# Where VectorE copies the second transposed block in a windowed attention: after the maxima of both heads, or between them

## The reference

```python
proj = h @ w_in                      # q: 16 heads of 64, k and v: 4 heads of 64, z: 1024
s = einsum(q, k) / 8                 # blocks of 128 queries against the block before and their own
s = where(in_band, s, -inf)          # diff >= 0 and diff < 128
m = maximum(max(s), sink)            # one sink per head
p = exp(s - m)
p = p / (sum(p) + exp(sink - m))
o = einsum(p, v)
return (o * silu(z)) @ w_out
```

## Time and profile before

| | |
|---|---|
| time, median of 3 runs | 1680.35 us (1679.25 to 1680.95) |
| time of the profiled execution | 1681.84 us |
| its span, first to last instruction | 1680.0 us |
| PE busy | 1616.8 us (96%) |
| DVE busy | 935.2 us (56%) |
| ACT busy | 707.2 us (42%) |
| slots i = 2 to 7 | 84.35 to 157.06 us of the span, six of 12.12 us |

### The profile page before, as it was taken

One profiled execution on the slowest core, in us unless ns is written; L12 is line 12 of the kernel. 1 busy time (PEld: TensorE's weight loads), 2 busy tenths in 40 slices (PEclk: granted clock), 3 DMA queues, 4 the chain that ended last, 5 costly groups with the idle time before them and its releaser, 6 DMA issues.

```text
span 1680.0 us, 20851 instructions
## 1 busy us (share of the span) xinstructions
PE 1616.8 (96%) x7745; PEld 1290.7 (77%) x7745; DVE 935.2 (56%) x1583; ACT 707.2 (42%) x1268; POOL 139.1 (8%) x131
## 2 busy tenths in 40 slices
PE   5998999999999999999999999999999999999998
PEld 4866888877778567888888888778566888888886
DVE  6566557566666765543434346566766643434343
ACT  4356532545544654422323244454664532323232
POOL 3000222031500001100000011000000200000001
PEclk8999999999999999999999999999999999999999
DMA  4211223323121101333333232211201232333331
GB/s 135 85 40 51 86 90 101 100 88 101 51 76 51 51 26 54 110 101 101 100 99 101 75 100 91 85 51 51 76 26 51 93 109 76 104 97 100 100 100 50
DMA packets 127271, 135.62 MB, mean 81 GB/s; under 512 B 2442, under 2 KB 120788, under 8 KB 127188
## 3 DMA queue, kind: packets, MB, share of 16 engines
q1 hardware_dynamic: 126084, 133.19, 24.7%
q0 software_dynamic: 288, 1.05, 0.2%
q10 hardware_dynamic: 816, 0.30, 0.1%
HBM read 132.43 MB, written 2.10 MB: 80 GB/s over the span
## 4 chain that ended last, share of the span: by engine, by line
PE 75%; DVE 14%; ACT 5%; issue 4%; DMA 1%; POOL 1%; SPq 0%; DVEq 0%; POOLq 0%; ACTq 0%
PE U L1228 21%; PE U L1230 21%; PE U L1229 21%; DVE cc L914 3%; PE Z L1406 3%; PE O L1460 2%; DVE ea L916 2%; DVE ea L911 1%; DVE pr L815 1%; PE U L1271 1%; PE U L1272 1%; PE U L1273 1%; DVE pr L833 1%; DMA raw<-in_attn_w_in 1%; PE O L1454 1%
## 5 line engine op out<-in xcount | busy, mean ns | idle before, releaser
L1228 PE MATMUL U<-XH,WL 128*128 128x512 f32 x976 | 386.3, 396 | 6.1 <-issue 5.2
L1230 PE MATMUL U<-XH,WH 128*128 128x512 f32 x976 | 381.3, 391 | 0.0
L1229 PE MATMUL U<-XL,WH 128*128 128x512 f32 x976 | 380.9, 390 | 0.0
L765 DVE TENSOR_TENSOR WL<-raw,WH 128x1024 fp32r<-128x1024 f32 x246 | 313.2, 1273 | 62.4 <-ACT WH L500 55.8
L500 ACT ACTIVATE WH<-raw 128x1024 fp32r<-128x1024 f32 x246 | 257.1, 1049 | 210.9 <-PE U L1230 173.6
L1228 PE MATMUL U<-MH,WL 128*128 128x512 f32 x848 | 335.7, 396 | 1.9 <-DVE tb L1097 1.7
L1230 PE MATMUL U<-MH,WH 128*128 128x512 f32 x848 | 330.8, 390 | 0.0
L1229 PE MATMUL U<-ML,WH 128*128 128x512 f32 x848 | 330.1, 389 | 0.0
L1228 PEld LDWEIGHTS U<-XH,WL 128*128 128x128 f32 x976 | 183.9, 188 | 44.6 <-issue 7.0
L1230 PEld LDWEIGHTS U<-XH,WH 128*128 128x128 f32 x976 | 183.7, 188 | 38.9
L1229 PEld LDWEIGHTS U<-XL,WH 128*128 128x128 f32 x976 | 184.0, 189 | 36.2
(11 more groups left out here) (219 smaller groups left out, 1756.4 us busy)
## 6 DMA issues: line engine op xcount, KB each, us to landing
raw<-in_w_ff SPq DMA_DIRECT2D x64, 1024.0 KB, 5.2
raw<-in_w_in SPq DMA_DIRECT2D x24, 1024.0 KB, 5.1
raw<-in_attn_w_in SPq DMA_DIRECT2D x10, 1024.0 KB, 5.3
raw<-in_pool_w_in SPq DMA_DIRECT2D x8, 1024.0 KB, 5.4
raw<-in_w_o SPq DMA_DIRECT2D x8, 1024.0 KB, 5.2
raw<-in_attn_w_out SPq DMA_DIRECT2D x4, 1024.0 KB, 5.0
raw<-in_pool_w_out SPq DMA_DIRECT2D x4, 1024.0 KB, 5.1
xin<-in_x SPq DMA_DIRECT2D x2, 1024.0 KB, 7.8
```

Source lines behind the costliest of these rows:

```text
L765: v.tensor_tensor(w_slot(WL, t, shape), src, w_slot(WH, t, shape).bitcast(F32), ALU.subtract).then_inc(lo_done, 1)
L1228: mm(o, wl, xh, start=first, stop=False, **kw)
L1229: mm(o, wh, xl, start=False, stop=False, **kw)
L1230: return mm(o, wh, xh, start=False, stop=last, **kw)
```

## The change

VectorE's copy of the second round of transposes moves from behind the maxima of both heads to between them: first the maxima of head 0, then the copy, then the maxima of head 1. No instruction is added or removed; the wait on the negated maxima of both heads and the release of the scores' PSUM stay behind head 1.

```diff
-            def swa_softmax_a(st):
+            def swa_softmax_a(st, heads):
                 j = st["pair"]
                 dve.wait_ge(z_done, st["zd"] + 1)
                 if j >= 2:
                     dve.wait_ge(p0_done, swa_t_of[j - 2]["p0"] + 4)
-                for i in range(2):
+                for i in heads:
...
-                dve.wait_ge(negm_ready, 2 * j + 2)
-                dve.sem_inc(z_free, 1)
+                if 1 in heads:
+                    dve.wait_ge(negm_ready, 2 * j + 2)
+                    dve.sem_inc(z_free, 1)
...
                 if "swa_qk" in by_op:
-                    swa_softmax_a(by_op["swa_qk"])
+                    swa_softmax_a(by_op["swa_qk"], [0])
                 if "swa_t" in by_op:
                     swa_evict(by_op["swa_t"], 1)
+                if "swa_qk" in by_op:
+                    swa_softmax_a(by_op["swa_qk"], [1])
                 conv(s["t"] + 2)
```

## The result

The changed kernel takes 1687.5 us in the median of 5 runs (1684.54 to 1689.87), the kernel before beside it 1680.35 us (1678.42 to 1681.16): 7.2 us more, a ratio of 1.005 with a 95% interval of 1.0039 to 1.0062. The direction was as forecast, the size was not: 4.3 us and at most 1686.8 us had been predicted. A second set of runs, made with the experiments, gave 1690.13 against 1678.87 us (1.0069, 1.0056 to 1.0082).

A forecast was written before the change was run, and what follows sets the result against it. The prediction took VectorE's ordered list, not TensorE, to set the slots' pace. Six slots of 0.72 us gave 4.3 us, so 1680.35 became 1684.7 us, 0.26% slower; the range was 1683.2 to 1686.8.

The forecast's parts named there:

- The ring: First-layer slots 2 to 7: 3.50 us of TensorE, then 8.62 us of VectorE's gapless list, close the 12.12 us period.
- VectorE's wait: Before the moved copy: VectorE stands 0.72 us for the second round of transposes, in each of six slots.
- Slot 1: First slot with transposes, no product with v: no new VectorE wait, its end stays, cost zero.
- The period: Time of one of slots 2 to 7: from 12.12 to 12.84 us.
- the 0.16 us wait on the negated maxima: VectorE's existing gap at the second round's copy: moves along unchanged, to in front of the weight remainder.
- the sum: Six slots of 0.72 us make 4.3 us; slot 1 and the last slot add 0.
- TensorE's path: Second path, via the late fourth round: TensorE free 0.61 to 0.77 us later, close to VectorE's 0.72.
- the lower of my two figures: TensorE's time from the fourth round until free for the product with v: 1.80 us, or 0.16 less.
- Where the gain goes: The third round's 0.70 us wait vanishes, but the fourth waits about 2 us for ScalarE's copy, 0.18 before.
- The clock: Rival: the 2.0 us TensorE gap lowers the clock; 1686 for one fall, up to 1705; chance 0.03.
- a sign that it is wrong: In the changed profile: a period of 12.12 us or less, or a fall of the clock, would refute the prediction.
- The price of one fall: Last part and product with v behind the gap, half or all at half speed: 1.7 to 3.4 us.

The follow-up runs named there:

- e3_later: Kernel before, with VectorE's copy of the second round moved between the second and third maximum of head 1; 1679.93 us, 1.0008 of before.
- e9_fill1: Changed kernel with 1 additional matmul in TensorE's gap before the fourth round, in seven slots; 1682.93 us, 1.0032 of before.
- e2_third_early: Changed kernel with ScalarE's copy of the third round placed between the exponentials of head 0 and head 1; 1688.28 us, 1.0058 of before.
- e6_after_rem: Changed kernel with VectorE's weight remainder, in slots with scores, moved behind the result of the tile; 1688.02 us, 1.0055 of before.
- e1_fill: Changed kernel with 8 additional matmuls in TensorE's gap before the fourth round, in seven slots; 1685.27 us, 1.0043 of before.
- The three filled kernels: Changed kernel with 8, 3 or 1 additional matmuls in TensorE's gap before the fourth round; 1685.27, 1683.48 and 1682.93 us.
- e4_rem: Kernel before, with VectorE's weight remainder, in slots with scores, moved behind the result of the tile; 1678.61 us, 1.0000 of before.
- e10_v3_slot1: As e5_rem_v3, but the weight remainder of the first slot with scores (i = 0) stays in its old place; 1675.76 us, 0.9986 of before.
- e5_rem_v3: As e4_rem, with VectorE instead of ScalarE copying the third round, between the two heads' normalisations; 1677.66 us, 0.9992 of before.

## Why the prediction missed

**The ring and VectorE's wait: right.** VectorE waits for the second round in every one of the six slots; 0.71 us measured, 0.72 worked out, and e3_later takes it away. Slot 1 costs 0.12 us (11.38 against 11.26), where I had nothing; the remainder starts later there too.

**The period: a term too small.** I took the 0.16 us wait on the negated maxima as moving along unchanged. The weight remainder behind it starts 0.42 us after the negation, not 0.33: 0.09 us a slot, 0.5 in all. The period was 12.94 us, forecast 12.84, and the sum 4.9 us instead of 4.3. The slot of the kernel before without a copy in that place, i = 0, would have shown it: there the remainder starts 0.41 us behind the negation (70.81 to 71.22).

**TensorE's path: right that there are two.** The fourth round's wait was forecast at about 2 us and is 2.02. The time from its start to the product with v is 1.84 us (91.25 to 93.09 in the changed kernel, 92.91 to 94.75 in e9_fill1), so the lower of my two figures, 1.64, was wrong and both chains end within hundredths of a microsecond. e2_third_early and e6_after_rem show each by itself.

**Where the gain goes: right.** The 0.70 us waits vanished and paid nothing, in the changed kernel as in e3_later.

**The clock: the step that failed.** The prediction priced it as a rival and said: "I take the nearer row, 1.50, so no fall. 0.03." The new gap of 2.0 us lay between a row of 1.50 without a fall and one of 2.80 with a fall, and I chose by nearness where the two ends differ by all or nothing. The row of 2.80 us was a weak witness besides: the clock there went down before that wait ended at 40.38, as the mean of 0.85 in this row of the kernel before shows:

```profile
39.00:40.00 1.00, 0.00 (x0) 0.00 (x0) 1.00 (x4) 0.00 (x0) 0.00 (x0) 0.85 0.02 8
```

So the cost of the clock stood in the sum at nothing, and the prediction had named a fall of the clock as a sign that it is wrong. The runs showed two falls in one profile and four in the other, 1.4 us each; e1_fill, which only keeps TensorE busy, takes 4.9 us less than the changed kernel. The three filled kernels have no fall in the slots and stand 4.7 to 6.4 us over before; the stated range, 2.9 to 6.4 us over, holds that. The price of one fall, 1.7 to 3.4 us, was too high. In the changed kernel the low clock lasted 3.4 us, and in it the way from the fourth round to the product with v took 2.81 us in place of 1.84 (117.12 to 119.93) and from there to the scores 2.13 in place of 1.66 (119.93 to 122.06). But a fall comes up to four times in the stretch, where I allowed one in the range. What the prediction cited from the Trainium skill ("TensorE: Matmul & The Clock Gate", section "HAM oscillation"), that an idle gap puts the clock back and that this can come again in every round of a loop, these profiles bear out for gaps of 2.0 us, in two to four of seven rounds and not in each.

Taken together: 4.9 us of period and two to four falls, 2.8 to 5.6 us, give 7.7 to 10.5; the two sets of runs measured 7.2 and 11.3. Both lie up to 0.8 us outside, which medians of five runs that scatter over some 5 us do not contradict.

## What to carry to other kernels

Before an earlier place for an instruction is taken for free, ask when its input is there. VectorE's ordered list was itself the ring's bound, so the changed kernel paid the wait at its head in full; e3_later, two maxima further down, paid 0.15 us a slot in place of 0.82. Removing a wait of TensorE does not remove idle time while something else sets the period; the idle time is collected elsewhere, and several short gaps that become one long one can cost the clock as well. A gap between a size seen harmless and one seen harmful is an open question with its own chance and price, and a fill of one to three matmuls can settle it. Where two chains of one length close a loop, both have to be made shorter: here the first alone gave 0.24 us a slot (e4_rem), both together 0.44 (e10_v3_slot1).

## What was not expected of the hardware

- The clock held behind gaps of 1.77 to 1.90 us that came once in 12.94 us, and fell behind some, not all, of gaps of 2.00 to 2.12 us of the same period. The length of one gap does not decide alone: a single gap of 2.49 us in e4_rem passed without a fall, and one of 2.47 us in e5_rem_v3 had a fall behind it.
- One fall of the changed kernel lasted from about 117.5 to 120.9 us at 0.50 and cost 1.41 us.
- In the kernel before the clock fell at 592.65 us although TensorE had been busy since 586.88 by its modelled ends, with attention products of 64 rows or 64 columns for most of that time. Why was not tried.
- Adding TensorE work shortened the kernel: 8 idle-filling matmuls in each of seven slots gave 4.9 us back, with one matmul in each the kernel stood 4.7 us over before, where the changed kernel stood 11.3 us over.
- VectorE's first instruction behind a wait on its own last result started 0.33 us after the start of that one when that was a copy out of PSUM and 0.42 us when it was the weight remainder, which waits on three further semaphores. Whether these waits are the cause was not tried.
